# The order in which GpSimd issues two streams of expert gathers

## The reference

```python
u_rows = jnp.take(U, e_b, axis=0)
act = jax.nn.gelu(jnp.einsum('tkd,td->tk', u_rows, x_b)) * g_b
v_rows = jnp.take(V, e_b, axis=0)
return jnp.einsum('tk,tkd->td', act, v_rows)
```

## Time and profile before

| | |
|---|---|
| median of 3 runs | 4069.53 us (4062.77 to 4085.47) |
| the profiled execution | 4059.65 us, span 4057.9 us |
| busy: TensorE, VectorE, GpSimd, ScalarE | 74%, 74%, 59%, 21% of the span |
| DMA | 345 GB/s mean; gathers' queue 69.6% of 16 engines' time, SyncE's queue 21.0% |
| gathers of u and of v | 1024 each, mean 1165 and 1156 ns on GpSimd |

### The profile page before, as it was taken

One profiled execution on the slowest core, in us unless ns is written; L12 is line 12 of the kernel. 1 busy time (PEld: TensorE's weight loads), 2 busy tenths in 40 slices (PEclk: granted clock), 3 DMA queues, 4 the chain that ended last, 5 costly groups with the idle time before them and its releaser, 6 DMA issues.

```text
span 4057.9 us, 42806 instructions
## 1 busy us (share of the span) xinstructions
PE 3001.7 (74%) x11794; PEld 1710.7 (42%) x11794; DVE 3009.5 (74%) x6485; ACT 866.6 (21%) x1753; POOL 2408.2 (59%) x2129
## 2 busy tenths in 40 slices
PE   6757788778776787778776787778776777753776
PEld 3743455336542455335532455336532455211431
DVE  2458876789569886789578876789579976788582
ACT  1111211322121311321121312221121212220112
POOL 1017775677556774577556774677556774575541
PEclk8778889989999899989999899989899899986778
DMA  5069999999999999999999999999999999998975
GB/s 163 31 222 389 348 362 384 398 375 354 376 347 416 349 370 373 374 372 359 374 360 416 347 372 360 385 369 363 365 354 416 341 377 369 372 351 307 357 273 209
DMA packets 453893, 1399.82 MB, mean 345 GB/s; under 512 B 44129, under 2 KB 55681, under 8 KB 453650
## 3 DMA queue, kind: packets, MB, share of 16 engines
q0 software_dynamic: 297216, 1082.26, 69.6%
q1 hardware_dynamic: 156434, 314.66, 21.0%
HBM read 1386.84 MB, written 9.93 MB: 344 GB/s over the span
## 4 chain that ended last, share of the span: by engine, by line
DVE 32%; PE 31%; DMA 16%; issue 12%; ACT 5%; PEld 2%; POOL 1%; DVEq 0%; SPq 0%; ACTq 0%; PEldq 0%; POOLq 0%
PE peer_acc L1038 10%; DVE uring L1737 7%; DMA wbuf<-in_peer_wq_dram 5%; PE bank L795 4%; DMA wbuf<-in_w_in_dram 4%; DVE accv L1730 4%; DMA wbuf<-in_w_out_dram 3%; PE bank L900 2%; PE bank L953 2%; DMA vring<-in_peer_v_dram,eidx 2%; PE bank L951 2%; PEld bank L900 1%; PE bank L955 1%; PE bank L756 1%; PE bank L1015 1%
## 5 line engine op out<-in xcount | busy, mean ns | idle before, releaser
L700 POOL DMA_INDIRECT uring<-in_peer_u_dram,eidx x1024 | 1193.2, 1165 | 947.1 <-issue 532.9
L712 POOL DMA_INDIRECT vring<-in_peer_v_dram,eidx x1024 | 1183.9, 1156 | 606.1 <-PE peer_acc L1038 306.3
L1038 PE MATMUL peer_acc<-vring,dg 128*128 128x512 f32 x2368 | 1229.2, 664 | 375.6 <-ACT dg L1086 340.2
L1737 DVE CUSTOM_DVE_ANT_0 uring<-uring,px 128x1024 f32<-128x1024 f32 x1024 | 1239.9, 1222 | 52.5 <-DMA uring<-in_peer_u_dram,eidx 21.1
L1038 PEld LDWEIGHTS peer_acc<-vring,dg 128*128 128x128 f32 x2368 | 473.8, 211 | 964.1 <-issue 641.1
L795 PE MATMUL bank<-wbuf,xT 128*128 128x512 f32 (+3 forms) x1440 | 665.1, 606 | 195.3 <-DMA wbuf<-in_w_in_dram 117.9
L1730 DVE SCALAR_TENSOR_TENSOR accv<-vring,pact,accv 128x1024 f32<-128x1024 f32 x424 | 545.2, 1286 | 71.9 <-DMA vring<-in_peer_v_dram,eidx 44.3
L795 PEld LDWEIGHTS bank<-wbuf,xT 128*128 128x128 f32 (+1 forms) x1440 | 262.9, 191 | 591.1 <-issue 279.0
L900 PE MATMUL bank<-xT,wbuf 128*128 128x128 f32 (+1 forms) x2304 | 299.8, 289 | 60.7 <-DMA wbuf<-in_peer_wq_dram 58.1
L900 PEld LDWEIGHTS bank<-xT,wbuf 128*128 128x128 f32 x2304 | 292.3, 208 | 85.0 <-DMA wbuf<-in_peer_wq_dram 68.9
L1086 ACT ACTIVATE dg<-ident,pact 128x128 f32<-128x128 f32 x592 | 200.4, 392 | 507.3 <-DVE pact L1718 498.7
(11 more groups left out here) (296 smaller groups left out, 3229.6 us busy)
## 6 DMA issues: line engine op xcount, KB each, us to landing
wbuf<-in_w_in_dram SPq DMA_DIRECT2D x198, 512.0 KB, 10.8
wbuf<-in_peer_wq_dram SPq DMA_DIRECT2D x144, 512.0 KB, 9.6
wbuf<-in_w_out_dram SPq DMA_DIRECT2D x72, 512.0 KB, 10.5
wbuf<-in_ple_gate_w_dram SPq DMA_DIRECT2D x72, 512.0 KB, 7.0
uring<-in_peer_u_dram,eidx POOLq DMA_INDIRECT x1024, 7.5
vring<-in_peer_v_dram,eidx POOLq DMA_INDIRECT x1024, 7.6
wbuf<-in_ple_w_dram SPq DMA_DIRECT2D x18, 512.0 KB, 12.3
ms<-in_shift_mu_dram SPq DMA_DIRECT2D x9, 896.0 KB, 12.0
```

The lines of the kernel that those rows point to most:

```text
L700: gp.indirect_dma_start(uring[:, s, :], None, peer_u, expert_rows(n, j)).then_inc(sig(f"u{s}_full"), 16)
L712: gp.indirect_dma_start(vring[:, s, :], None, peer_v, expert_rows(n, j)).then_inc(sig(f"v{s}_full"), 16)
L1038: last = mm(acc[c][:, :], dg[:, n % 2, at, :], vring[:, s, c * 512:(c + 1) * 512], start=(n + at == 0), stop=(n == UNITS - 1 and j == pe_e ...
L1737: v.tensor_tensor_reduce(out=uring[:, s, :], in0=uring[:, s, :], in1=px[:, :], scale=1.0, scalar=0.0, op0=ALU.mult, op1=ALU.add, accum_out ...
```

## The change

In GpSimd's `expert` the issue of v is moved against that of u. Before, a unit n issued v(n, 0-1) at its second expert and v(n, 2-3) at its fourth, each behind a pair of u of unit n+1. Now it issues v(n-1, 2-3) at the second expert and v(n, 0-1) at the fourth; the last unit issues its own v(31, 2-3) as well, since no unit follows.

```diff
--- before.py
+++ after.py
@@ -725,9 +725,15 @@
                     if j % 2:
                         gather_u(i, n + 1, j - 1)
                         gather_u(i, n + 1, j)
-                if j % 2:
-                    gather_v(i, n, j - 1)
-                    gather_v(i, n, j)
+                if j == 1 and n:
+                    gather_v(i, n - 1, 2)
+                    gather_v(i, n - 1, 3)
+                if j == 3:
+                    gather_v(i, n, 0)
+                    gather_v(i, n, 1)
+                    if n == UNITS - 1:
+                        gather_v(i, n, 2)
+                        gather_v(i, n, 3)
 
             def peer_sample():
                 gp.wait_ge(sig("handed"), NB + 1)
```

## The result

The changed kernel takes 4103.69 us, median of 7 runs (4089.96 to 4119.73), beside 4069.53 us for the kernel before (7 runs, 4053.51 to 4085.47). The ratio is 1.0092, 95% interval 1.0065 to 1.0118: slower by 0.9%, where 0.58% was forecast. The profiled execution took 4089.96 us, its span 4088.2 us. In code of the changed kernel lines behind the change are 6 higher: L1021 is L1015 of before, L1743 L1737, L1044 L1038.

A forecast was written before the change was run, and what follows sets the result against it. Bound by full DMA engines for 120 us of a pass, then by GpSimd's pace; 6 x 3.5 + 2.5 = 23.5 us on the profiled 4059.65 us, 0.58%, gives 4093 us on the median; range 4042 to 4116 us.

The forecast's parts named there:

- Where a u slot sets the clock, v loses: From the 8.92 us GpSimd wait through the full-DMA stretch: u keeps its place, each v comes four gathers later.
- 3.5 us a pass: End of the full-DMA stretch, six loop passes: VectorE through at 1780.1 instead of 1776.6, TensorE's parallel delay not added.
- The lower end: Full-DMA stretch, v late by only two gathers: 0.2 to 1 us a pass, 4076 us in all; chance 0.25.
- the cover: VectorE's wait for ScalarE, 1774.3 to 1776.58, at the end of the full-DMA stretch: said to hide 2.3 us of delay.
- Where a v slot set it, cost 0 and gain 0: From unit 11, after GpSimd's 5.55 us v-slot wait: v keeps its place, u comes four gathers earlier, buying nothing.
- the relieved wait counts: Rival: u gathers issued inside GpSimd's wait for TensorE gain 3.0 us in seven passes; 4028 to 4049 us; chance 0.21.
- Both regimes lose: Rival: in 1797 to 1960 u slots hold GpSimd too, v late there, 5 us a pass more; 4128 us; chance 0.09.
- The weights take the turn: Rival: in the full-DMA stretch fewer queued gathers let TensorE's weights land sooner, at most 2.5 us a pass; 4052 us; chance 0.05.
- First and last pass: First pass, v late with DMA full: 2.5 us lost; last pass, paced by GpSimd and the sample's loads: 0.

The follow-up runs named there:

- the two halves: New order in units 6 to 10 alone and in units 0 to 5 alone, each against the kernel before: ratios 1.0049 and 1.0062.

## Why the prediction was right or wrong

*Where a u slot sets the clock, v loses: right.* The u waits kept their places, v(6,3) was issued at 1741.50 (1741.51 predicted), v(7,2) at 1751.36 (1752.63) and v(8,3) at 1764.75 (1766.58). The v gathers that after issued from 1745 to 1785 landed (us from issue, min, median, max)

```profile
DMA to landing us min/median/max: 8.2/10.9/12.1
```

where 11.0 was used. The step "two gathers fewer are behind it than now, and the DMA engines, which had drained, can't make that up in a stretch in which they are full" is shown by the new order in units 0 to 5 alone: 2.06 gathers are missed, and v(7,2) lands 2.9 us late at the end of the stretch. One thing in it was off: the gathers are missed over the turn of the pass, mostly ahead of its first row, and not at the 8.92 us wait. That v is late by four gathers, two lost and two by the order, is shown by the two halves, 2.9 us late each and 5.2 us together. The times add up too: 0.62% and 0.49% come to 1.11%, and units 0 to 10 together cost 1.06%.

*3.5 us a pass: right in size, for this pass 2.6 on VectorE and 3.0 on TensorE.* The six passes lost 25.7 us in the profiled pair, 21.0 was the term. The second to the sixth lost 2.6 to 3.8 us by unit 11, the seventh 8.8. The seventh is the pass in which TensorE ran the burst at the full clock before and largely at the low one after. In the kernel with the new order in units 4 to 10 it is the sixth that loses 7.5 us, with a burst of 5.89 us and 3.57 us of wait for ScalarE. So a part of the size is the clock's, which the prediction doesn't have, and that the sum came near is in that part luck.

*The lower end was wrong.* The text had it that if v were late by two gathers and not four, "after the cover of 2.3 us next to nothing is left". Two gathers late is what the new order in units 6 to 10 and that in units 0 to 5 each make, and they cost 0.49% and 0.62%, 20 and 25 us on 4062.68, where 3.7 to 8.5 us were priced. The step that failed is "That wait is the cover, and it hides 2.3 us". VectorE waits there for ScalarE, ScalarE for TensorE, and how long TensorE takes hangs on its clock: in five of the six loop passes of before the burst took 5.8 to 6.3 us and the wait was there, in the sixth it took 3.72 us and there was none. With v two gathers late, the passes in which VectorE hardly waited for ScalarE lost 0.3 to 1.3 us by unit 11, about what the lower end had; those in which the wait came back behind the late v lost 3.3 to 4.3 us. Whether a late v brings the low clock or chance does, no run shows, since none holds the clock fixed. Over whole runs the mean granted clock is 0.878 in the changed kernel and 0.888 in the kernel before.

*Where a v slot set it, cost 0 and gain 0: right within 0.3%.* New order from unit 11 on is at 0.9984, the hole filled and the relieved wait gone. In its profiled execution the loop is faster,

```profile
742.87 5.89 PE bank L1029 x8
...
3460.27 5.38 PE bank L1029 x8
```

2717.4 us against 2730.4, though it begins 9.3 us later. So the rival *the relieved wait counts* may have some 2 us a pass in that execution, where 3.0 were priced, and the runs leave 0.01 to 0.31%. By unit 11, ahead of the moved gathers, two of its passes are already 2 us ahead, so not all of it is the relieved wait.

*Both regimes lose: wrong.* A u wait of 2.23 us did come at unit 11, but v(11,0) behind it has 0.71 us of idle time ahead of it, where 5.55 us stood, and is issued 1.5 us later, less than the 2.6 us that VectorE is late by then. With the new order from unit 11 on alone nothing is lost.

*The weights take the turn: they landed sooner, and it was worth nothing.* For the pieces of the full stretch whose landing the trace has, 22 before and 16 after, the median from issue to landing fell from 12.2 to 9.9 us. TensorE's waits for them fell from 117.9 to 62.6 us, and it then waited for v, 111.3 us more. The prediction had read the Trainium skill, DMA: Bandwidth & Descriptors, Queues, rings and completion order (engines take turns between the queues that have work), as speaking against sooner weights as long as gathers are queued. They were queued all through (their queue took 75.6% of the engines' time in this stretch before and 75.5% after), and the weights came sooner all the same. That doesn't mean that fewer queued gathers did it: with the new order in units 0 to 5, where a v gather took 14.1 us to land, the median of the weights is 10.0 us. TensorE takes the pieces at other times in these kernels, so they are issued at other times too; no run tells the two causes apart.

*First and last pass.* The first lost 5.8 us in the profiled pair where 2.5 was the term. With the new order in parts of the pass it lost 0.2 to 7.0 us, so a single pair doesn't size it. The last pass lost nothing in its experts, as forecast (its dots are 27 us late at the second unit and 25 at the last); 5 us more come in what follows them, where other kernels show 0 to 5 us. The cause is open.

The sum of 23.5 us stands against 30.3 us between the two profiled executions and 34.2 us between the medians.

## What to carry to other kernels

A gather that stands directly ahead of its use doesn't tolerate another one being put before it, even when the other one's wait seems to be what binds: look first at who waits for the result. A wait for a third engine covers a delay only as long as that engine takes what it took in the trace; find out what the cover itself hangs on, here TensorE's clock, and look at it in every pass and not in one. And where DMA engines are full for long, what they miss before stays missing for that whole stretch (120 us here), so keep the queue filled at its head.

## What was not expected of the hardware

Halving each u row takes 1024 x 0.262 MB = 268 MB of the 1399.82 MB that the kernel moves, 19%, and made it only 1.7% faster (0.9828). Full as the DMA engines are for 120 us of each pass, a gather of u costs GpSimd no less with half the bytes (mean 1181 ns, was 1165), and the waits for u slots stay (379.3 us in all, was 401.8).

One and the same burst of 16 matmuls took 3.72 us in one pass and 5.6 to 6.5 us in another of the same execution, by TensorE's granted clock, and with it came or went a wait two engines further on. And v(13,3) took 3.58 us on GpSimd in most loop passes and 8.3 us in some, where the gathers around it took 0.9 to 2 us.
